# PEER experts: TensorE's products with low parts last, U split ahead of a wait on ScalarE, and SyncE's loads reordered

## The reference, cut to what matters

```python
def _peer(h, wq, keys, u_tab, v_tab):
    ...
        e = i1 * N_KEYS + i2
        g = jax.nn.softmax(cv, axis=-1)
        a = jax.nn.gelu(jnp.einsum('td,thkd->thk', tb, u_tab[e]).astype(jnp.float32), approximate=False)
        return jnp.einsum('thk,thkd->td', (g * a).astype(tb.dtype), v_tab[e])
```

## Time and profile before

| quantity | value |
|---|---|
| median of 3 runs | 4041.88 us (4033.55 to 4056.06) |
| the profiled execution, its time | 4036.62 us |
| its span in the profile | 4034.8 us |
| TensorE busy | 3311.0 us, 82% |
| VectorE busy | 2778.2 us, 69% |
| GpSimd busy | 1709.0 us, 42% |
| ScalarE busy | 1357.6 us, 34% |
| first and last L2206 of the experts stage | 2029.2 and 3922.1 us |

### The profile page before, as it was taken

How to read it: one execution, slowest core, us unless ns; L and a number is a source line. 1 busy time by engine, 2 the same in 40 slices (tenths; PEclk the granted TensorE clock), 3 DMA queues, 4 the chain that set the end, 5 groups by cost and what they waited for, 6 DMA issues and landing times. The chain is left out here.

```text
span 4034.8 us, 59078 instructions
## 1 busy us (share of the span) xinstructions
PE 3311.0 (82%) x20585; PEld 2890.3 (72%) x20585; DVE 2778.2 (69%) x5881; ACT 1357.6 (34%) x3190; POOL 1709.0 (42%) x1341
## 2 busy tenths in 40 slices
PE   6999688566686892666589999999999999999994
PEld 3677455211376792555489999999999999999993
DVE  3223676100231199999779998999999889999885
ACT  3010466000221111887633333333333333333331
POOL 1010000000212441888765665665565565565560
PEclk7999799777788996776699999999999999999997
DMA  6632546999422331787598998998988988898983
GB/s 232 221 124 74 172 148 212 357 412 406 161 72 77 99 115 42 200 240 205 141 329 318 330 325 303 326 331 311 326 319 314 334 316 314 320 322 307 328 300 148
DMA packets 389552, 1001.89 MB, mean 248 GB/s; under 512 B 187044, under 2 KB 232975, under 8 KB 325688
## 3 DMA queue, kind: packets, MB, share of 16 engines
q1 hardware_dynamic: 323768, 491.18, 35.9%
q0 software_dynamic: 62656, 469.86, 32.2%
q10 hardware_dynamic: 2944, 38.77, 2.6%
HBM read 914.75 MB, written 152.04 MB: 264 GB/s over the span
## 5 line engine op out<-in xcount | busy, mean ns | idle before, releaser
L2174 DVE CUSTOM_DVE_ANT_0 e_uv<-e_uv,e_h 128x1024 f32<-128x1024 f32 x416 | 721.7, 1735 | 73.8 <-DMA e_uv<-peer_uv,k_g_idx 73.1
L2243 POOL DMA_INDIRECT e_uv<-peer_uv,k_g_idx x416 | 521.1, 1253 | 540.4 <-DVE e_pY L2186 496.8
L1475 PE MATMUL e_po<-e_ph,e_vh 128*128 128x320 f32 x2048 | 646.3, 316 | 59.2 <-DVE k_OT L2218 55.1
L1475 PE MATMUL e_pa<-k_hi_d,e_uh 128*128 128x320 f32 x2048 | 638.4, 312 | 50.7 <-POOL e_ul L2234 37.5
L1476 PE MATMUL e_po<-e_pl,e_vh 128*128 128x320 f32 x2048 | 633.3, 309 | 0.0
L1477 PE MATMUL e_po<-e_ph,e_vl 128*128 128x320 f32 x2048 | 633.3, 309 | 0.0
L1477 PE MATMUL e_pa<-k_hi_d,e_ul 128*128 128x320 f32 x2048 | 633.2, 309 | 0.0
L1476 PE MATMUL e_pa<-k_lo_d,e_uh 128*128 128x320 f32 x2048 | 633.1, 309 | 0.0
L2186 DVE SCALAR_TENSOR_TENSOR e_pY<-e_uv,e_wts,e_pY 128x1024 f32<-128x1024 f32 x412 | 526.0, 1277 | 0.0
L1475 PEld LDWEIGHTS e_po<-e_ph,e_vh 128*128 128x128 f32 x2048 | 384.8, 188 | 83.7 <-DVE k_OT L2218 71.3
L1475 PEld LDWEIGHTS e_pa<-k_hi_d,e_uh 128*128 128x128 f32 x2048 | 384.8, 188 | 62.0 <-issue 46.0
(11 more groups left out here) (305 smaller groups left out, 5889.7 us busy)
## 6 DMA issues: line engine op xcount, KB each, us to landing
k_kv<-kv_pages SPq DMA_DIRECT2D x128, 512.0 KB, 7.0
s_kv<-kv_state SPq DMA_DIRECT2D x32, 2048.0 KB
e_v<-peer_uv SPq DMA_DIRECT2D x128, 512.0 KB
e_u<-peer_ut SPq DMA_DIRECT2D x126, 512.0 KB, 6.1
s_g<-r_G SPq DMA_DIRECT2D x10, 4096.0 KB
k_OT<-s_g SPq DMA_DIRECT2D x128, 320.0 KB
v_win_sample<-state_v_win POOLq DMA_DIRECT2D x28, 1168.0 KB, 10.0
k_win_sample<-state_k_win ACTq DMA_DIRECT2D x28, 1168.0 KB
```

The lines of the kernel that those rows point to most:

```text
L1475: nc.tensor.matmul(out, lhs_hi, rhs_hi, start=start, stop=False)
L2174: nc.vector.tensor_tensor_reduce(uv[:, r, 0:D], uv[:, r, 0:D], h[:], 1.0, 0.0, ALU.mult, ALU.add, dots[:, r:r + 1]).then_inc(row_dotted, 1)
L2243: nc.gpsimd.indirect_dma_start(uv[:, s % RING], None, io["peer_uv"], bass.IndirectOffsetOnAxis(ap=keep.g_idx[:, s:s + 1], axis=0),).then_i ...
```

## The change

On TensorE the waits and the order of the matmuls within a group change, not their number. A dot starts when the high part of U is there, does its 16 products with it, and then waits for the low part (only at b = 0). `out` likewise starts with the high parts of V and of the products, four matmuls, then takes the four with V's low part and then the four with `e_pl`. On ScalarE `split_u` of blocks 2 and 3 moves from behind the copy to `e_ph` to between gelu and the wait for `p_done`. On SyncE the loop now goes over quads, with U of blocks 2 and 3 of the next quad loaded at the end of the loop's body.

```diff
-                with sp.Fori(0, NK // 2 - 1) as i:
-                    for u in range(2):
-                        c = 2 * i + u
-                        sp.wait_ge(ul_done, c + 1)
-                        sp.dma_start(uu[:, u], uview[ds(c + 2, 1)].rearrange("a p k e -> (a p) k e")).then_inc(u_in[u], 16)
-                        sp.wait_ge(p_done, NBD * c + NBD + 2)
-                        sp.dma_start(G[:, u], row(io["s_g"], c + 2)).then_inc(g_in[u], 16)
-                        sp.wait_ge(vl_done, c + 1)
-                        sp.dma_start(vv[:, u], row(vview, c + 2)).then_inc(v_in[u], 16)
+                def load_u(i, c):
+
+                    sp.wait_ge(ul_done, CQ * i + c - 1)
+                    sp.dma_start(uu[:, c % 2], uview[ds(CQ * i + c, 1)].rearrange("a p k e -> (a p) k e")).then_inc(u_in[c % 2], 16)
+
+                def load_g(i, c):
+
+                    sp.wait_ge(p_done, NBD * (CQ * i + c - 1) + 2)
+                    sp.dma_start(G[:, c % 2], row(io["s_g"], CQ * i + c)).then_inc(g_in[c % 2], 16)
+
+                def load_v(i, c):
+                    sp.wait_ge(vl_done, CQ * i + c - 1)
+                    sp.dma_start(vv[:, c % 2], row(vview, CQ * i + c)).then_inc(v_in[c % 2], 16)
+
+                for c in (2, 3):
+                    load_u(0, c)
+                with sp.Fori(0, NQ - 1) as i:
+                    for load, c in ((load_v, 2), (load_g, 2), (load_u, 4), (load_v, 3), (load_g, 3), (load_u, 5), (load_g, 4),
+                                    (load_v, 4), (load_v, 5), (load_g, 5), (load_u, 6), (load_u, 7)):
+                        load(i, c)
...
                 def dot(i, c):
-                    pe.wait_ge(ul_done, CQ * i + c + 1)
+                    pe.wait_ge(uh_done, CQ * i + c + 1)
                     for b in range(NBD):
                         m = NBD * c + b
                         pe.wait_ge(p_done, DOTS * i + m + 1)
                         cols = slice(b * WD, (b + 1) * WD)
                         for k in range(KC):
-                            x = split_product(nc, pa[:, m % 2, 0:WD], uh[:, c % 2, k], ul[:, c % 2, k],
-                                              keep.hi_d[:, k, cols], keep.lo_d[:, k, cols], k == 0, k == KC - 1)
+                            nc.tensor.matmul(pa[:, m % 2, 0:WD], uh[:, c % 2, k], keep.hi_d[:, k, cols], start=(k == 0), stop=False)
+                            nc.tensor.matmul(pa[:, m % 2, 0:WD], uh[:, c % 2, k], keep.lo_d[:, k, cols], start=False, stop=False)
+
+                        if b == 0:
+                            pe.wait_ge(ul_done, CQ * i + c + 1)
+                        for k in range(KC):
+                            x = nc.tensor.matmul(pa[:, m % 2, 0:WD], ul[:, c % 2, k], keep.hi_d[:, k, cols], start=False,
+                                                 stop=(k == KC - 1))
                         x.then_inc(dotted, 1)
...
                 def out(i):
-                    pe.wait_ge(vl_done, CQ * i + CQ)
+                    pe.wait_ge(vh_done, CQ * i + CQ)
...
-                        pe.wait_ge(pl_done, DOTS * i + NBD * (CQ - 2) + b + 1)
+                        pe.wait_ge(ph_done, DOTS * i + NBD * (CQ - 2) + b + 1)
...
+                                nc.tensor.matmul(po[:, n % SUMS, 0:WD], vh[:, c, rows], ph[:, c, cols], start=(c == 0), stop=False)
+
+                            if n == 0:
+                                pe.wait_ge(vl_done, CQ * i + CQ)
...
+                            if k == 0:
+                                pe.wait_ge(pl_done, DOTS * i + NBD * (CQ - 1) + b + 1)
...
                     nc.scalar.activation(pa[:, m % 2, 0:WD], pa[:, m % 2, 0:WD], ACT.Gelu).then_inc(gelu_done, 1)
+                    if b == 1 and c < 2:
+                        split_u(CQ * i + 2 + c)
                     act.wait_ge(p_done, n + 3)
...
                         gelus(i, m)
-                        if m % NBD == 1 and m // NBD < 2:
-                            split_u(CQ * i + 2 + m // NBD)
                         if m in V_AT:
                             split_v(CQ * i + V_AT.index(m))
```

More of the change, by code:

```diff
@@ L2038, in _ @@
                     sp.dma_start(G[:, u], io["s_g"][u]).then_inc(g_in[u], 16)
-                with sp.Fori(0, NK // 2 - 1) as i:
-                    for u in range(2):
-                        c = 2 * i + u
-                        sp.wait_ge(ul_done, c + 1)
-                        sp.dma_start(uu[:, u], uview[ds(c + 2, 1)].rearrange("a p k e -> (a p) k e")).then_inc(u_in[u], 16)
-                        sp.wait_ge(p_done, NBD * c + NBD + 2)
-                        sp.dma_start(G[:, u], row(io["s_g"], c + 2)).then_inc(g_in[u], 16)
-                        sp.wait_ge(vl_done, c + 1)
-                        sp.dma_start(vv[:, u], row(vview, c + 2)).then_inc(v_in[u], 16)
+                def load_u(i, c):
[13 more added lines that the diff above has]
+                        load(i, c)
+                for load, c in ((load_v, 2), (load_g, 2), (load_v, 3), (load_g, 3)):
+                    load(NQ - 1, c)
             @block.tensor
@@ L2075, in out @@
                                 if k == 0 and c == CQ - 1:
-                                    pe.wait_ge(pl_done, DOTS * i + NBD * (CQ - 1) + b + 1)
-                                x = split_product(nc, po[:, n % SUMS, 0:WD], vh[:, c, k * P:(k + 1) * P],
-                                                  vl[:, c, k * P:(k + 1) * P], ph[:, c, cols], pl[:, c, cols],
-                                                  c == 0, c == CQ - 1)
+                                    pe.wait_ge(ph_done, DOTS * i + NBD * (CQ - 1) + b + 1)
+                                nc.tensor.matmul(po[:, n % SUMS, 0:WD], vh[:, c, rows], ph[:, c, cols], start=(c == 0), stop=False)
+                            if n == 0:
+                                pe.wait_ge(vl_done, CQ * i + CQ)
+                            for c in range(CQ):
+                                nc.tensor.matmul(po[:, n % SUMS, 0:WD], vl[:, c, rows], ph[:, c, cols], start=False, stop=False)
+                            if k == 0:
+                                pe.wait_ge(pl_done, DOTS * i + NBD * (CQ - 1) + b + 1)
+                            for c in range(CQ):
+                                x = nc.tensor.matmul(po[:, n % SUMS, 0:WD], vh[:, c, rows], pl[:, c, cols], start=False,
+                                                     stop=(c == CQ - 1))
                             x.then_inc(summed, 1)
```

1 line of the change is left out of this document (added).

## The result

| | before | after |
|---|---|---|
| median | 4045.75 us of 4 runs (4033.55 to 4056.06) | 4127.93 us of 4 runs (4121.59 to 4134.38) |
| profiled execution, its span | 4036.62, 4034.8 us | 4121.59, 4119.8 us |

The ratio is 1.0204 (1.017 to 1.0238): the change makes the kernel 82 us slower. (The kernel before has one run more here than in the table ahead of the prediction.) The direction was forecast; 4128 lies outside the range of 4016 to 4092.

A forecast was written before the change was run, and what follows sets the result against it. The loop through VectorE, ScalarE and GpSimd was taken as the bound, with TensorE's waits slack. Terms 0, +1.05 and -0.45 gave +0.60 us a quad, times 31 +19 us, forecast 4060 us; 8-in-10 range 4016 to 4092.

The forecast's parts named there:

- TensorE's order: Experts stage: up to 17 us of waits on e_ul go, but nobody waits for the earlier dot; booked 0.
- again without anybody behind it: Seventh half on TensorE: a later product adds a wait on VectorE of about a microsecond, with nobody waiting behind it.
- ScalarE's early split: U's split ahead of the wait at m = 3: e_ul starts 1.1 us earlier, costing +1.05 us a quad.
- The walk: Quad followed start by start from m = 3: e_pl waits for e_ul, everything behind ends 1.05 us late.
- one pair: First quad: a subtraction issued inside a row dot took 2.64 us, and the next e_pl 2.67 instead of 0.48.
- +1.63: Upper end for the early split, per quad: the subtraction starts just ahead of the row dot, which is itself held.
- SyncE's order: New load order: a 0.82 us gather wait goes, U of block 3 costs about 0.4; net -0.45 us a quad.
- half a collision: U of block 3 lands in front of the next gather and takes about half of the 0.82 us wait, 0.4.
- the upper bound: SyncE's loads: +0.82 us a quad if U costs what the collision before cost and nothing is won.
- The 0.50 us of V's late load: V's next split waited 0.50 us for its load; the earlier issue removes that, leaving the split 1.05 us late.
- the slower end: Rival, U in front of the gathers: each quad 1.87 us longer, +58 us, 4100; slower cases together 0.20.
- its variant with the held dot: Slower case with the row dot itself held: +1.63 and -0.45 us a quad, 4078; slower cases together 0.20.

The follow-up runs named there:

- pe_alone: The kernel before with TensorE's new order and nothing else; 4036.60 us in one run, 4030.55 before.
- act_back: The changed kernel with ScalarE's split of U put back, so TensorE's order and SyncE's loads new; 4074.63 us, 1.0110 of the kernel before.
- sp_alone: The kernel before with SyncE's new order of loads alone; 4070.75 us in one run, 4030.55 before.
- gated_pe_old: The kernel before with U's two splits of the output part earlier and their subtractions waiting for a finished row dot; 3974.38 us, 0.9832 of before.
- low_u_waits: The changed kernel, but GpSimd starts the subtraction of m = 3 only when e_pl of m = 3 is done; 4078.89 us, 1.0115 of the kernel before.
- act_alone: The kernel before with ScalarE's earlier split of U alone; 4059.04 us in one run, 4039.76 before.
- low_u_first: The changed kernel with GpSimd's subtraction of m = 3 moved to m = 2, ahead of the gathers; 4116.11 us in one run, 4035.99 before.
- u3_late: TensorE's and SyncE's new orders, ScalarE as before, U of block 3 loaded in the next quad behind G of block 2; 4073.97 us, 1.0088 of before.

## Why the prediction was right in direction and wrong in size

**TensorE's order: booked 0, measured 0.** Its waits were slack in the loop of before (pe_alone), in that of the new loads (act_back against sp_alone) and in the faster one (gated_pe_old); in the changed kernel itself its order was not put back alone. The test "who waits for TensorE" gave the right answer. But "again without anybody behind it" was wrong: with the wait for the product grown to 79.1 us, gelus waited 26.2 us for TensorE, most of it at m = 6 and 7. With the same order of TensorE and the row dot free (low_u_waits) it is 11.0, so this is an echo of the held row dot. Against the 9.1 of before it is at most 17 us, and it lies inside the cost of the next term.

**ScalarE's early split: booked 1.05, measured 1.43.** This is the first step that failed. The walk assumed that the subtraction, issued inside a running row dot, waits for it and makes `e_pl` pay. That was read from one pair, in which GpSimd had idled for 4.28 us and was released by a split that ended inside the row dot:

```profile
2036.73 1.06 ACT L2093 ACTIVATE e_uh<-e_u 128x1024 fp32r<-128x1024 f32 x1
```

that is 0.75 us after the row dot's start at 2037.04. In the changed kernel the split ends 2.1 us before the row dot starts (the prediction itself has 3002.2 against 3004.20), and the row dot pays. The last section shows that this order decides in every case recorded. The start of the subtraction was right: it came at the gather's recorded end, and the 0.3 us that the prediction allowed for a longer gather did not appear. The bound for that, +1.63, was in the text, with a condition ("just ahead of the row dot") that doesn't fit the recorded starts: 0.5 us inside counts too. The step behind m = 3 grew by 2.6 us; some 1.2 of it come back behind, since the next row dots are less held, and 1.43 remain. With the pairing of the forecast (act_alone) the cost in the dots part is 1.04. So the working of the dots part was right, and its choice between two ends was not. That the whole kernel paid only 0.66 a quad there, the output part being 0.38 shorter, the walk didn't see. The sum should have had as a rival the held row dot with the price of the upper end on its own, not only beside a gain on the loads.

**SyncE's order: booked -0.45, measured +0.82 in the output part and +0.24 in the dots part.** This is the second step that failed, and the larger one (1.5 us a quad). The expected gain at the ninth row dot came. The price of U in front of a gather had been put at half a collision (0.4); in the changed kernel the step with the tenth row dot grew by 1.52 us (1.69 in sp_alone), four times that, while the one with the ninth shrank by 0.81, where 0.82 was expected. The output part's +0.82 equals the upper bound, by luck: that bound had the old wait stay and a new one of 0.82 come, and what came in the changed kernel is 0.81 less and 1.52 more, with small shifts beside. For the dots part there was no term at all. The 0.50 us of V's late load was counted as lying on the loop. Behind it stood the hold of a subtraction on the next operation, and taking the wait away only moved the hold on (read from the rows of sp_alone). So the direction was right only because the cost of the split was put above a gain on the loads that wasn't there.

**The range.** The other two terms came out near the upper ends that the text gives: 1.43 under +1.63, and 0.82 + 0.24 over +0.82. The two ends together are 2.45 us a quad, times 31 is 76 us, which on 4036.6 is 4113; the profiled run had 4121.6. The two ends had been priced in separate rivals (1.05 with 0.82, 1.63 with -0.45), and the range ended at 4092, below both together. Nor were they independent: the earlier U is what lets the split end before the row dot starts, so that the subtraction wins (act_alone, 35 waits for U's load). Nearest to what happened were the slower end and its variant with the held dot, but each was priced with the mild value of the other term.

**What would show it.** Of the signs of the forecast, the waits of TensorE changed as said, the row dot behind `e_pl` fell from 1.99 to 1.33 us on average, and the gelu at m = 5 came 2.1 us later behind the product of m = 3 (1.6 were named). A long `e_pl` at m = 3 (0.48) and a smaller idle time of VectorE did not come. Signs of rivals came, each by half: a short `e_pl`, but with `e_ul` 0.9 us behind the product and not 2; gelus waiting for TensorE 26.2 us, as an echo; and long waits for gathers in most quads, but only one of them behind n = 4, at the tenth row dot (over 0.8 us in 31 quads), the other at n = 1, at the seventh (27 quads).

## What to carry to other kernels

Before an operation is moved earlier on an engine that can hold another one up, look at what the other engine runs at the new time, and at which of the two is ready first: here the same 2.4 us subtraction costs nothing beside an addition with an input in PSUM and up to 2.8 us beside a row dot, and placing it behind a finished row dot, together with the earlier splits, won 1.5% where starting it sooner lost about 1% (1.43 us a quad). A load that comes late can be what keeps two long operations from running back to back, and a bulk load issued beside a gather can be paid by the gather: 1.8 us a quad here. When several terms of a sum have ends of their own, the range has to hold them together, above all when one edit sets the condition for the other.

## What the runs showed of the hardware

**What is ready first holds the other.** In the fourteen traces 78 subtractions are recorded as starting inside a row dot (five more, in low_u_first, follow another subtraction directly and are left out). In 32 the row dot was held (4.04 us in the row above): 29 in the changed kernel and 3 in act_alone. All 32 followed a gather by 0.01 to 0.02 us and started 0.51 to 0.53 us into the row dot. In the other 46 the subtraction was the one that waited. What GpSimd did just before doesn't separate them, since 12 of the 46, all in act_alone, also followed a gather by under 0.05 us and started 0.51 to 0.54 us into the row dot. What does is the end of ScalarE's split, which releases the subtraction: in all 32 it lies 0.13 us or more before the row dot's start (about 2.1 in the changed kernel), in all 46 at most 0.07 us before it, or after it. Between 0.07 and 0.13 us there is no case.

How far the row dot had come when it was stopped can be read from the end: in the 32 cases it ends 1.09 us after the subtraction's recorded end (3051.99 + 4.04 against 3052.50 + 2.43 in the rows above), and in 1860 cases of the fourteen traces in which the subtraction's recorded start lies ahead of the row dot's it ends 1.08 us after it (1845 of them within 1.07 to 1.10). So in the 32 it had done as little as in those: it stood still from its start on, half a microsecond before the recorded start of the subtraction, while the gather's record was still open. The gather by itself isn't the cause, since the same gather stands beside the unheld row dot of the earlier trace rows.

The Trainium skill, SBUF — State Buffer, section Who interferes with whom, says that a VectorE instruction with two SBUF inputs contends with a GpSimd instruction that reads SBUF, and that issue order decides who blocks. The trace agrees with the first (1.21 against 4.04 us). With the second it agrees if the order is taken from the release, the end of the split, and not from the recorded starts. The Trainium skill's Perfetto Trace Analysis, section GPSIMD Engine Instruction, calls GpSimd's spans unreliable and has the reported start at the read of one of its processors, after the instruction has begun there. That would fit; no run here shows it.

**A hold can last through several operations.** `e_pl`, 0.48 us by itself, took 5.69 us through what was left of three subtractions back to back (low_u_first): between them VectorE didn't get in.

**A load of 512 KB beside a gather.** The share of the DMA engines is 0.86 to 0.91 in the stage, and yet the place of one load decided 56 us of waits at one row dot (65.7 against 9.6 us in act_back and u3_late). The mean share says nothing about it.
